# A two-block transformer kernel: row norm factors taken off the inputs of the products and put on their outputs

## The reference

```python
def rms_norm(x, g):
    y = x * rsqrt(mean(x * x, axis=-1, keepdims=True) + 1e-6)   # a factor r[t] for each token
    return y * g                                                # a weight g[k] for each feature

hn = rms_norm(h, attn_pre_norm);  proj = hn @ w_in              # layer one, attention
hn = rms_norm(h, ffn_pre_norm);   u = causal_dwconv(hn @ w_up, conv_w, conv_b)
h  = rms_norm(h, ffn_norm);       (silu(h @ w_gate) * (h @ w_up)) @ w_down   # layers two and three
```

## Time and profile before

| | before |
|---|---|
| median of three runs | 2044.3 us (2043.35 to 2045.88) |
| the profiled execution: its own time | 2044.26 us |
| its span in the profile | 2042.5 us |
| granted TensorE clock, mean share | 0.972 |
| HBM read, mean over the span | 158.14 MB, 78 GB/s with the writes |
| POOL busy | 1105.1 us (54%) |
| ACT busy | 470.7 us (23%) |

### The profile page before, as it was taken

The page is one execution under the profiler, slowest core; times in us unless marked ns, Lnnn a source line. Parts: engine busy times, 40 slices in busy tenths (PEclk is TensorE's granted clock), DMA queues, the critical chain, the costliest instruction groups (busy, mean ns, idle before and its releaser), DMA issues.

```text
span 2042.5 us, 28343 instructions
## 1 busy us (share of the span) xinstructions
PE 1888.7 (92%) x10604; PEld 1537.1 (75%) x10604; DVE 785.3 (38%) x1174; ACT 470.7 (23%) x1164; POOL 1105.1 (54%) x714
## 2 busy tenths in 40 slices
PE   5776889799999989997999999998998899999999
PEld 4666657688888878764888888886886588888887
DVE  3776574554342034766332122004635542221100
ACT  2112553322221013445210011002225311110100
POOL 4436324376666655441556666655662456666663
PEclk9888899999999989999999999999999999999999
DMA  4223002132333322121132333222330023233232
GB/s 129 64 62 93 12 2 73 52 114 92 102 114 96 100 75 74 56 63 42 63 93 92 103 92 96 90 93 64 93 103 22 22 83 93 92 101 95 94 102 83
DMA packets 126693, 162.63 MB, mean 80 GB/s; under 512 B 12728, under 2 KB 88456, under 8 KB 126599
## 3 DMA queue, kind: packets, MB, share of 16 engines
q1 hardware_dynamic: 121697, 160.49, 25.3%
q10 hardware_dynamic: 4902, 0.82, 0.2%
HBM read 158.14 MB, written 2.10 MB: 78 GB/s over the span
## 4 chain that ended last, share of the span: by engine, by line
PE 84%; DVE 8%; ACT 3%; issue 2%; DMA 1%; POOL 1%; ACTq 1%; SPq 0%; DVEq 0%; POOLq 0%
PE ps L799 24%; PE ps L800 24%; PE ps L801 24%; PE ps L1154 3%; PE ps L814 1%; PE ps L930 1%; PE ps L1127 1%; DVE p_turn L2319 1%; PE ps L1201 1%; DVE nmax L2285 1%; DVE tok L2011 1%; ACT tok L1778 1%; PE ps L1217 1%; PE ps L1231 1%; DVE rstd L1987 1%
## 5 line engine op out<-in xcount | busy, mean ns | idle before, releaser
L454 POOL TENSOR_TENSOR w_lo<-raw,w_hi 128x1024 fp32r<-128x1024 f32 (+1 forms) x256 | 615.2, 2403 | 21.4
L452 POOL TENSOR_SCALAR w_hi<-raw 128x1024 fp32r<-128x1024 f32 (+1 forms) x256 | 276.2, 1079 | 517.2 <-PE ps L801 491.4
L799 PE MATMUL ps<-xt_hi,w_hi 128*128 128x512 f32 (+1 forms) x1160 | 432.6, 373 | 7.2 <-DVE xt_lo L2021 6.5
L800 PE MATMUL ps<-xt_lo,w_hi 128*128 128x512 f32 (+1 forms) x1160 | 432.0, 372 | 0.0
L801 PE MATMUL ps<-xt_hi,w_lo 128*128 128x512 f32 (+1 forms) x1160 | 431.9, 372 | 0.0
L799 PE MATMUL ps<-w_hi,xt_hi 128*128 128x512 f32 (+3 forms) x672 | 262.2, 390 | 22.8 <-ACT tok L1860 19.8
L800 PE MATMUL ps<-w_lo,xt_hi 128*128 128x512 f32 (+3 forms) x672 | 257.5, 383 | 0.0
L801 PE MATMUL ps<-w_hi,xt_lo 128*128 128x512 f32 (+3 forms) x672 | 257.3, 383 | 0.0
L799 PEld LDWEIGHTS ps<-xt_hi,w_hi 128*128 128x128 f32 x1160 | 218.9, 189 | 47.0 <-DVE xt_lo L2021 7.5
L801 PEld LDWEIGHTS ps<-xt_hi,w_lo 128*128 128x128 f32 x1160 | 218.8, 189 | 38.7
L800 PEld LDWEIGHTS ps<-xt_lo,w_hi 128*128 128x128 f32 x1160 | 218.9, 189 | 38.2
(11 more groups left out here) (319 smaller groups left out, 2243.4 us busy)
## 6 DMA issues: line engine op xcount, KB each, us to landing
raw<-in_w_up SPq DMA_DIRECT2D x88, 256.0 KB
raw<-in_l_w_gate SPq DMA_DIRECT2D x88, 256.0 KB
raw<-in_l_w_up SPq DMA_DIRECT2D x88, 256.0 KB
raw<-in_l_w_down SPq DMA_DIRECT2D x40, 512.0 KB
raw<-in_l_w_in SPq DMA_DIRECT2D x36, 512.0 KB
raw<-in_w_down SPq DMA_DIRECT2D x20, 512.0 KB
raw<-in_l_w_o SPq DMA_DIRECT2D x16, 512.0 KB
raw<-in_w_in SPq DMA_DIRECT2D x12, 512.0 KB
```

The costliest lines, as they stand in the source:

```text
L452: e.tensor_scalar(w_hi[:, s, 0:width], r, 1.0, 0.0, ALU.mult, ALU.add).then_inc(split, 1)
L454: e.tensor_tensor(w_lo[:, s, 0:width], r, w_hi[:, s, 0:width].bitcast(F32), ALU.subtract).then_inc(split, 1)
L799: e.matmul(o, s_hi, m_hi, start=start, stop=False)
L800: e.matmul(o, s_hi, m_lo, start=False, stop=False)
```

## The change

The factor `r[t]` of a row commutes with the product: `(h * r * g) @ w = r * ((h * g) @ w)`. The kernel after turns `h` itself, as soon as it is there. The gain `g[k]` is then a column on the partitions of the turned tile, and is applied in the two operations that empty it: ACT's copy to `xt_hi` takes it as its scale, and DVE's `xt_lo` becomes `scalar_tensor_tensor` (the PSUM bank times gain, minus `xt_hi`). The factor `r[t]` is applied to the results:

- in `in1`, `in2` and `in3` the tokens are on the partitions of the result, and ACT's copies out of PSUM take `rs`, `rs/8` or `-rs` as their scale instead of a constant. The two chunks of `in2` that come from normed latents stay as they were, and the forget gates take one more DVE multiplication;
- in the `up` stages the tokens lie along the free dimension. The four factors of a partition are written out to 128 by 512 (`wide_rs`), turned by four transposes into bank 7 and copied to SBUF (`rs_rows`), once a stage. Then DVE multiplies each of the 44 result banks of a stage by `rs_rows` in place, in PSUM (`scaled`), before ACT and DVE read it.

The order of the turning changes. For `n6`, `n7`, `n8` (and `n0`) the unit is a column: feature tile `k` of all four token tiles in one bank. The last column half of `out2`, `down2` and `out3` is no longer made in pairs of token tiles. The four feature tiles of the first column half are turned while the second half is still being multiplied, and the other four after the first slab of the following stage, whose first group or chunk now runs once over all 512 tokens. `n3` and `n5`, which stand behind a post norm, keep their pairs, with pieces of two feature tiles by two token tiles; after `down1` the post norm is done in place in PSUM, in halves. For `n0` all 32 transposes stand ahead of the first chunk, and wait for the whole of `x`.

The small tensors are laid out on the host into two arrays (`smalls`, 444 KB; `table`, 393 KB), beside the positions and the gains as columns (`g_pre`, 24 KB). SP loads them; `g_pre` stands behind `x`, the others between the second and the third slab of `w_in`. The broadcast loads of the six pre-norm gains, ACT's small loads and `turn_smalls` are gone. The sine table is made after `up1`. The product banks of `up2`, `up3`, `in3`, `out2`, `down2`, `out3`, `down3` are renamed (`UP_BANKS`, `OUT_BANKS`, `TOK_BANKS`).

```diff
+    def pe_turn_pair(e, name, p):
+        e.wait_ge(*at({"n3": "out1_res", "n5": "down1_res"}[name], 2 * p + 2))
+        for j in range(4):
+            for x in range(2):
+                for t in range(2):
+                    k = 2 * j + x
+                    m = e.transpose(bank(BY_PAIRS[name][4 * p + j], P, (2 * x + t) * P),
+                                    h[:, 2 * p + t, k * P:(k + 1) * P], ident[:, :])
...
+    def pe_turn_columns(e, name, half):
+        if name == "n0":
+            e.wait_ge(*at("h_full", 64))
+        else:
+            e.wait_ge(*at({"n6": "out2_res", "n7": "down2_res", "n8": "out3_res"}[name], NT * half + NT))
+        for k in range(4 * half, 4 * half + 4):
+            for t in range(NT):
+                m = e.transpose(bank(BY_COLUMNS[name][k], P, t * P), h[:, t, k * P:(k + 1) * P], ident[:, :])
+            m.then_inc(sem(f"{name}_tp"), 1)
...
+        if xt in BY_COLUMNS:
+            for s in range(4):
+                slab_there(0, s)
+                columns_there(s or 1)
+                for t in range(NT):
+                    m = tile(0, s, t)
+                m.then_inc(slab_used, 1)
+                if s == 0 and name == "in3":
+                    pe_turn_columns(e, xt, 1)
...
+    def pe_out_direct(e, name, there, norm):
+        for c in range(2):
+            for s in range(4):
+                e.wait_ge(split, 2 * (4 * (phases[name].g0 + c) + s) + 2)
+                if c == 0:
+                    e.wait_ge(*there[s])
+                for t in range(NT):
+                    m = slab_tile(e, name, c, s, OUT_KTS[s], x_model, KD - 1, t)
+                m.then_inc(slab_used, 1)
+                if c == 1 and s == 1:
+                    pe_turn_columns(e, norm, 0)
+    def pe_down(e, name, up, norm):
         e.wait_ge(*at(f"{up}_h", 20))
+        pe_slabs(e, name, 0, 0, DOWN_KTS, x_hidden, up)
+        if norm in BY_COLUMNS:
+            pe_slabs(e, name, 1, 0, DOWN_KTS[:3], x_hidden, up)
+            pe_turn_columns(e, norm, 0)
+            pe_slabs(e, name, 1, 3, DOWN_KTS[3:], x_hidden, up)
+        else:
+            pe_slabs(e, name, 1, 0, DOWN_KTS[:8], x_hidden, up)
+            pe_pairs(e, name, 1, 8, DOWN_KTS[8:], x_hidden, KF - 1, norm)
...
+        def scale_rows():
+            e.wait_ge(*at(f"{name}_wide", 1))
+            e.wait_ge(*at(f"{xt}_lo", KD))
+            for t in range(NT):
+                m = e.transpose(bank(7, P, t * P), wide_rs[:, t, :], ident[:, :])
+            m.then_inc(sem(f"{name}_bt"), 1)
...
+            for p, T in enumerate((slice(0, SEQ // 2), slice(SEQ // 2, SEQ))):
+                for s in range(4):
+                    if p == 0:
+                        e.wait_ge(split, 8 * g0 + (2 * s + 2))
+                    e.wait_ge(*at(f"{xt}_lo", 4 * p + s + 1))
+                    for j in range(4):
+                        if p == 0 and s == 0:
+                            e.wait_ge(*at(f"{xt}_lo", j + 1))
+                        m = first_tile(s, j, T)
+                    if p == 1:
+                        m.then_inc(slab_used, 1)
+                    if p == 0 and s == 2:
+                        pe_turn_pair(e, xt, 1)
+                    if p == 1 and s == 2:
+                        scale_rows()
...
+    def act_high(e, od, name, i):
+        e.wait_ge(*at(f"{name}_tp", i + 1))
+        for k, T, src in turned_piece(name, i):
+            op = e.activation(xt_hi[:, k, T], src, ACT.Copy, scale=gain_of(name, k))
+        op.then_inc(*od.done(*at(f"{name}_hi", i + 1)))
+    def act_norm(e, od, name):
         for t in range(NT):
+            if name == "n0":
+                e.wait_ge(*at("h_full", 64))
+            act_square(e, od, h[:, t, :], D, 2 * t, f"{name}_sq", t + 1)
+        act_rstd(e, od, name, 1, NT, 0, 2)
...
+    def dve_low(e, od, name, i):
+        e.wait_ge(*at(f"{name}_hi", i + 1))
+        for k, T, src in turned_piece(name, i):
+            op = e.scalar_tensor_tensor(out=xt_lo[:, k, T], in0=src, scalar=gain_of(name, k),
+                                        in1=xt_hi[:, k, T].bitcast(F32), op0=ALU.mult, op1=ALU.subtract)
+        op.then_inc(*od.done(*at(f"{name}_lo", i + 1)))
+    def dve_norm(e, od, name, up=None):
+        e.wait_ge(*at(f"{name}_sq", NT if name in WHOLE else 2 * NT))
         if name not in WHOLE:
+            e.tensor_tensor(ss[:, 0:2 * NT:2], ss[:, 0:2 * NT:2], ss[:, 1:2 * NT:2], ALU.add).then_inc(*od.own())
             e.wait_ge(*od.latest())
+        dve_rstd(e, od, name, 1, NT, D, 0, 2)
+        if up:
+            e.tensor_copy(wide_rs[:, :, :], rstd[:, 0:2 * NT:2].unsqueeze(2).broadcast_to([P, NT, P])).then_inc(
+                *od.done(*at(f"{up}_wide", 1)))
+            return
+        e.tensor_scalar(rs_less, rstd[:, 0:2 * NT:2], -1.0, None, ALU.mult).then_inc(*od.own())
+        e.tensor_scalar(rs_8th, rstd[:, 0:2 * NT:2], 0.125, None, ALU.mult).then_inc(*od.own())
+        e.tensor_copy(rs, rstd[:, 0:2 * NT:2]).then_inc(*od.done(*at(f"{name}_rs", 1)))
...
+    def dve_out(e, od, name, norm, up=None):
+        if name in POSTS:
+            gain_ready(e, name)
+            for p in range(2):
+                pair = (2 * p, 2 * p + 1)
+                e.wait_ge(*at(f"{name}_sq", NT + 2 * p + 2))
+                a = 8 + 4 * p
+                e.tensor_tensor(ss[:, a:a + 4:2], ss[:, a:a + 4:2], ss[:, a + 1:a + 4:2], ALU.add).then_inc(*od.own())
+                e.wait_ge(*od.latest())
+                dve_rstd(e, od, name, p + 1, 2, D, a, 2)
+                for t in pair:
+                    for c in range(2):
+                        half = out_half(name, c, t)
+                        e.scalar_tensor_tensor(out=half, in0=half, scalar=rstd[:, 8 + 2 * t:9 + 2 * t],
+                                               in1=gains[:, 0, c * W:(c + 1) * W], op0=ALU.mult,
+                                               op1=ALU.mult).then_inc(*od.own())
+                        e.wait_ge(*od.latest())
+                        cs = slice(c * W, (c + 1) * W)
+                        e.tensor_tensor(h[:, t, cs], half, h[:, t, cs], ALU.add).then_inc(
+                            *(od.done(*at(f"{name}_res", t + 1)) if c else od.own()))
+                for j in range(4):
+                    dve_low(e, od, norm, 4 * p + j)
+            dve_norm(e, od, norm, up)
...
+            def scaled(j):
+                if j == 3:
+                    e.wait_ge(slab_used, 4 * (gi + g0) + 4)
+                else:
+                    e.wait_ge(*at(f"{name}_acc", 3 * gi + (j + 1)))
+                b = bank(UP_BANKS[name][1 - even][j])
+                e.tensor_tensor(b, b, rs_rows, ALU.mult).then_inc(*od.done(*at(f"{name}_r", 4 * gi + (j + 1))))
...
+        e.wait_ge(*at(f"{name}_bt", 1))
+        e.tensor_copy(rs_rows, bank(7)).then_inc(*od.done(*at(f"{name}_bc", 1)))
...
+        e.dma_start(g_pre[:, :, :], A["g_pre"]).then_inc(sem("g_full"), 16)
+            sp_group(e, ph["in1"].g0, slabs[:2])
+            e.dma_start(smalls[:, :], A["smalls"]).then_inc(sem("small_full"), 16)
+            e.dma_start(pos_i[:, :], A["positions"]).then_inc(sem("small_full"), 16)
+            e.dma_start(table[:, :], A["table"]).then_inc(sem("small_full"), 16)
+            sp_group(e, ph["in1"].g0, slabs[2:], first=2)
...
-                    e.activation(tok3[:, t, 0:W], bank(EVEN[t]), ACT.Copy, scale=0.125).then_inc(*od.done(cp, last))
+                    e.activation(tok3[:, t, 0:W], bank(EVEN[t]), ACT.Copy, scale=rs_8th[:, t:t + 1]).then_inc(*od.done(cp, last))
```

More of the change, by code:

```diff
@@ L286, in build @@
     k_squares = gains[:, :, :].rearrange("p a (k n) -> p (a k) n", n=W)
-    xn = tok[:, 0:2 * D].rearrange("p (s n) -> p s n", s=2)
+    rope_c, rope_s = (table[:, x * NT * HD:(x + 1) * NT * HD].rearrange("p (t d) -> p t d", t=NT) for x in range(2))
+    w2_sb = table[:, 2 * NT * HD:3 * NT * HD].rearrange("p (k x d) -> p k x d", k=2, x=2)
+    rs, rs_8th, rs_less = (row_scale[:, x, :] for x in range(3))
+    wide_rs = tok[:, 0:NT * P].rearrange("p (t n) -> p t n", t=NT)
+    rs_rows = gains[:, 1, 0:W]
     half_u = tok[:, 0:4 * W].rearrange("p (s n) -> p s n", s=4)
@@ L934, in first_chunk @@
[L934 to L953 removed]
+    def out_bank(name, c, t):
+        return OUT_BANKS[name][c][t]
@@ L976, in pe_slabs, with pe_pairs @@
             m.then_inc(slab_used, 1)
-    def pe_pairs(e, name, c, s0, kts, x_of, last, turn, when):
+    def pe_pairs(e, name, c, s0, kts, x_of, last, norm=None):
         phase = phases[name]
@@ L990, in pe_pairs @@
                     m.then_inc(slab_used, 1)
-                    for t in when.get(s - s0, ()) if turn else ():
-                        turn(t)
-    def pe_out_direct(e, name, there, turn_next, when):
-        for s in range(4):
-            e.wait_ge(split, 2 * (4 * phases[name].g0 + s) + 2)
-            e.wait_ge(*there[s])
-            for t in range(NT):
-                m = slab_tile(e, name, 0, s, OUT_KTS[s], x_model, KD - 1, t)
-            m.then_inc(slab_used, 1)
```

(33 more changed lines are left out.)

700 lines of the change are left out of this document (293 added, 407 removed).

## The result

The changed kernel takes 2022.36 us (median of four runs, 2021.07 to 2023.12), the kernel before 2045.09 us (four runs, 2043.35 to 2047.01). The ratio is 0.9888, 95% interval 0.9871 to 0.9905: 22.7 us faster. The forecast was 1982 us with a range of 1972 to 2000; the time lies 40 us above the forecast and 22 above the end of the range. The profiled execution took 2022.13 us, its span is 2020.4.

What follows compares the result with a forecast made beforehand. PE, busy 92% of the span, bounds the kernel, so time falls only where it waits, runs cold or overpays a step. 31.2 + 5.9 + 7.5 + 4.9 + 5.8 + 6.0 = 61.3 us off 2044.3 gives 1983, stated 1982; own range 1976 to 1989, wider 1972 to 2000.

Steps and rivals of the forecast that it cites:

- the sum: All stages: gains at the start, n3, n5, n6, n7 and n8 add up to 61.3 us.
- 0.224 us a step: PE in a stretch without a norm: 1450 matmuls in 325.0 us, no gap, at the full granted clock of 2.4 GHz.
- scaled: Up stages: DVE's 44 bank multiplications a stage, 0.69 us each, 2.8 a group, covered by PE's 21.5 us a group.
- Start: n0 and in1: second chunk begins at 37.5 instead of 67.25, row factors at 25; 31.2 us won, bounds 24 and 33.
- n3: After out1: PE waits only for h, first group 6.0 us earlier; 5.9 us won, bounds 3 and 8.
- n5: After down1: transposes begin 6.5 us earlier, new 4 us wait for the second pair; 7.5 us won, bounds 4 and 10.
- n6, n7, n8: Norms turned by columns: waits for xn and xt_lo or cold steps go; 4.9, 5.8 and 6.0 us, bounds 3 and 7.
- rival (d): Up stages: DVE's multiplications in PSUM make DVE the bound, so slower, 2112 us at 4 us each; chance 0.02.
- The scales on ACT's copies replace constants: 0: ACT's copies out of PSUM: taking a scale in place of a constant adds 0 us.
- Rival (a): Start and norms: new waits eat half of the gain, 40 us remain, 2004 us; chance 0.15.
- (c): in1: the start is hidden anyway, its 31 us return as waits before the compression, 30 us remain, 2014 us; chance 0.06.

Runs made afterwards that it cites:

- experiment 1: Kernel after with two small tiles (384 B) ahead of h, so the weight tiles lie where the kernel before had them: 1982.95 us, ratio 0.9703 to before.
- realigned kernel: The kernel of experiment 1: kernel after with h, raw, w_hi and w_lo back at the addresses of the kernel before, no instruction changed: 1982.95 us.
- Experiment 11: Realigned kernel with ACT's row squares of tiles 0 and 1 made before its copies of the second pair, effective after down1 only: 1983.00 us, ratio 0.9695.
- Experiment 10: Realigned kernel with PE's first product waiting for n0's row factors: 1996.72 us; or with the first column half of n6, n7, n8 turned behind the last slab: 1992.62 us.
- Experiment 4: Kernel after with each of DVE's 132 multiplications of a PSUM bank by the row factors done on one column instead of 512: 2023.6 us.
- experiments 1 to 8: Spare tiles moved, added or resized in the kernel before, after or realigned kernel, shifting operand addresses: 1982.95 to 2080.53 us; Experiment 4 instead cut DVE's multiplications.

## Why the prediction was wrong

**The step that failed** is one that the sum doesn't even show: it priced every matmul at the step of the kernel before ("0.224 us a step"; since 30 of the 1450 of the earlier trace rows are of half width, a full one is really 0.2267), and the changed allocations at nothing. The diff shows the line `sb("align_h", [P, 96])` removed and `sb("align_x", [P, ALIGN])` added. The kernel after pays 6.2 ns more on each of 6384 matmuls, 39.4 us (experiment 1). I said that what the change adds (`scaled`, the scales on ACT's copies, the sine table) lies beside other work; no rival had a price for a PE step that changes. No row of the kernel before could give that price; that the weight tiles move could be seen. With that one term the sum is 61.3 - 39.4 = 21.9 us, and 22.7 were measured.

**The rest of the working, read on the realigned kernel** (span 1981.4, 61.1 us less than before; the sum said 61.3). That the sum comes out to 0.2 us is chance, since its terms are off by up to 4.6 us in both directions:

- Start: 32.0 us at the end of `in1`, forecast 31.2. PE's first product is at 15.64 there (15.5 said) and the second chunk's first at 37.53 (37.5 said). The row factors are there at 29.8 and not 25, since DVE's small steps beside POOL took 2 us instead of 0.2 several times, but before 33 as needed.
- n3: 5.4 us at the end of `up1`, forecast 5.9. The first product came 6.3 us sooner (6.0 said), and the wait of 0 to 2.5 us ahead of the second pair's transposes did not come. But PE waits 1.8 us for `wide_rs`, of which I had counted the transposes alone (DVE's copy into it took 2.49 us, beside a POOL split of 2.36, as I had said it could); it is the one wait in the `up` stages, where I had said there would be none.
- n5: the first product of `in2` came 7.7 us sooner and the second half's first 6.8 (7.5 said), but the end of `in2` only 2.9. This term was mis-sized: I followed the chain up to the second half pass and not to the emptying of the first chunk's banks. ACT's first copy needs `rs`. In the kernel after, DVE, POOL and ACT:

```profile
752.22 2.38 POOL L471 TENSOR_TENSOR w_lo<-raw,w_hi 128x1024 fp32r<-128x1024 f32 x1
...
752.38 2.25 DVE L1998 TENSOR_SCALAR row_scale<-rstd 128x4 f32<-128x4 f32 x1
...
754.87 0.58 ACT L1879 ACTIVATE tok<-ps,row_scale 128x384 f32<-128x384 f32 x1 [5.72 <-DVE row_scale L2000]
```

  Four squares, rstd and three DVE steps follow the last `xt_hi`; ACT waits 5.72 us for them, and then PE waits 2.4 for its bank and runs at its lower clock (granted 0.50) for eight steps of about 0.43 us. Three of the DVE steps take 1.96, 0.97 and 2.25 us instead of 0.16 to 0.2; each begins during an operation of POOL's splits and ends with it (752.38 + 2.25 = 754.63, beside 752.22 + 2.38 = 754.60). I had a price for such collisions at the start, and none here. Experiment 11 confirms that the late factors are the cause: there the stage is 4.1 us shorter. But it changed two things at once. Two squares came sooner, by 2.4 us, and the DVE steps ended before POOL's first split (734.03), so that the chain behind the last square took 1.6 us, where the realigned kernel has 6.6:

```profile
733.57 0.17 DVE L2002 TENSOR_SCALAR row_scale<-rstd 128x4 f32<-128x4 f32 x1
...
734.03 1.05 POOL L469 TENSOR_SCALAR w_hi<-raw 128x1024 fp32r<-128x1024 f32 x1 [15.71 <-PE ps L810]
```

- n6, n7, n8: 6.4, 6.1 and 6.4 us, forecast 4.9, 5.8 and 6.0, with no wait for `h`. Experiment 10 puts 7.5 of these 18.9 us down to the early turning.
- These add up to 59.2. Of the last 1.9, 1.4 lie in the attention of layer three, 80.4 us at a granted clock of 0.98 before and 78.9 at 1.00 here.
- `scaled`: 132 of 0.70 us, forecast 0.69, and covered, as said. Experiment 4 excludes rival (d).
- "The scales on ACT's copies replace constants: 0" was wrong for the instruction: a copy of 128x512 with a scale per partition takes 0.69 us where the earlier trace rows has 0.60. The Trainium skill ("ScalarE: Activation LUTs", "What ACT_TABLE_LOAD costs") says that each such operand adds about 93 ns. The trace agrees, with 689 against 597 ns. ACT, busy 24% of the span, hides it.

Rival (a) gave 2004 by new waits that eat gains; those that were not forecast cost 4.8 us in `in2` and 1.8 in `up1`. That 2022 lies nearest to (c)'s 2014 is chance: the start was not hidden.

## What to carry to other kernels

A change of the allocations is a change of the kernel. Compare the start-to-start step of the commonest matmul in equal windows of both traces before looking at any wait, and when it moved, compare operand addresses. Here a spare tile with "align" in its name carried 39 us, more than the 23 that the change as a whole brought. Whoever removes such a spare must keep the distance, here modulo 256 bytes, between the two operands of each matmul. When a whole run is slower or faster by a few us, compare the granted clock of its stages before naming a cause: the two runs of experiment 10 are 9.7 and 13.6 us longer in total, and 7.5 and 11.9 at the place of the edit. Look, too, in the trace whether an edit took effect where it was meant to; in experiment 11 it did so at one of two norms. And when row factors move from the inputs to the outputs, the new deadline is the emptying of the first bank: follow the chain to it.

## What the runs showed of the hardware

- The full-clock step of a 128x512 fp32 matmul is 0.2267 us when the weight tile and the other operand's tile lie a multiple of 256 bytes apart within the partition (six placements), and 0.2324 to 0.2333 at 32 and 128 bytes off; at 64 bytes it is 0.2333 in four stages and 0.2289 to 0.2301 in the others (experiments 1 to 8). The Trainium skill ("TensorE: Matmul & The Clock Gate", "Wait — 56ns, not 53.3ns?") has 215.7 ns for this size. Neither level here is as low, and no run shows why.
- DVE steps on 128x4 values take 0.16 to 0.2 us alone and up to 2.3 us beside POOL's splits, as `row_scale` above: they end together with the POOL operation that was running when they began.
- The length of attention follows the granted clock: 88.1 us at 0.96 and 91.0 at 0.92, 78.9 at 1.00 and 81.6 at 0.96, and between `in1` and `out1` 145.4 at 0.91 and 147.6 at 0.87, for the same instructions. That is enough to hide a gain of 4 us.
